# Four of a block's 123 weight splits moved from VectorE to GpSimd, in the first two attention slots of a decoder layer

## The reference

```python
mod = silu(c) @ ada_w + ada_b                       # shift, scale and gate of both halves
h = rms_norm(x, norm1_g) * (1 + scale1) + shift1
proj = h @ w_in                                     # attention q,k,v | deltanet q,k,v,beta,decay,z | gate A | gate D
o_attn = sliding_window_attention(q, k, v, sinks)   # window 128, 8 query heads, 2 key heads of 64
o_dn = gated_delta_rule(...)                        # 4 heads of 128; needs T = inverse(L + eye), L strictly lower
merged = sigmoid(gate_a) * (o_attn @ w_branch[A]) + sigmoid(gate_d) * (o_dn @ w_branch[D])
x = x + gate1 * (merged @ w_out)
h = rms_norm(x, norm2_g) * (1 + scale2) + shift2
x = x + gate2 * ((silu(h @ w_gate) * (h @ w_up)) @ w_down)
```

## Time and profile before

| what | value |
|---|---|
| median of three runs | 3070.0 us (3067.14 to 3070.06) |
| the profiled execution's own time | 3071.86 us |
| its span, first to last instruction | 3070.1 us |
| mean granted TensorE clock | 0.992 of full speed |
| TensorE matmul busy | 3010.6 us (98%) |
| VectorE / ScalarE / GpSimd busy | 53% / 39% / 4% |

### The profile page before, as it was taken

The page is one execution under the profiler, slowest core; times in us unless marked ns, Lnnn a source line. Parts: engine busy times, 40 slices in busy tenths (PEclk is TensorE's granted clock), DMA queues, the critical chain, the costliest instruction groups (busy, mean ns, idle before and its releaser), DMA issues.

```text
span 3070.1 us, 39395 instructions
## 1 busy us (share of the span) xinstructions
PE 3010.6 (98%) x15656; PEld 2477.8 (81%) x15656; DVE 1615.7 (53%) x2589; ACT 1211.3 (39%) x1980; POOL 114.1 (4%) x110
## 2 busy tenths in 40 slices
PE   7999999999999999999999999999999999999999
PEld 4887878888788788888879778888887977878887
DVE  4876565433466657333365756633336575643333
ACT  3654533222255544322245644422224554432222
POOL 0011000000001100000000110000000011000000
PEclk9999999999999999999999999999999999999999
DMA  6543344333434343333343344333334333323333
GB/s 250 162 151 100 127 158 151 96 96 100 134 104 127 98 130 115 105 96 96 97 137 123 97 116 143 102 98 97 96 95 137 128 107 100 124 83 96 96 96 103
DMA packets 138582, 358.30 MB, mean 117 GB/s; under 512 B 38304, under 2 KB 38560, under 8 KB 135328
## 3 DMA queue, kind: packets, MB, share of 16 engines
q1 hardware_dynamic: 134048, 347.40, 35.3%
q10 hardware_dynamic: 4352, 8.39, 0.7%
HBM read 326.38 MB, written 29.36 MB: 116 GB/s over the span
## 4 chain that ended last, share of the span: by engine, by line
PE 82%; DVE 7%; issue 4%; ACT 3%; DVEq 2%; DMA 1%; SPq 1%; POOL 0%; POOLq 0%; ACTq 0%
PE gb L1771 66%; PE gb L1800 4%; PE gb L2132 4%; PE mb L1977 2%; DVE w_lo L1152 1%; DVE tmp_c L1463 1%; DVE inv_c L1466 1%; PE mb L1972 1%; ACT sc L944 1%; PE mb L1950 1%; PE mb L1883 1%; ACT sc L936 1%; PE mb L2043 0%; DMA ada_buf<-in_ada_w 0%; PE gb L1782 0%
## 5 line engine op out<-in xcount | busy, mean ns | idle before, releaser
L1771 PE MATMUL gb<-h_hi,w_hi 128*128 128x512 f32 x2432 | 960.5, 395 | 18.6 <-DVE w_lo L1152 11.6
L1771 PE MATMUL gb<-h_hi,w_lo 128*128 128x512 f32 x2432 | 958.1, 394 | 0.0
L1771 PE MATMUL gb<-h_lo,w_hi 128*128 128x512 f32 x2432 | 958.1, 394 | 0.0
L752 ACT ACTIVATE w_hi<-w_raw 128x1024 fp32r<-128x1024 f32 x492 | 518.6, 1057 | 1040.7 <-PE gb L1771 981.3
L1152 DVE TENSOR_TENSOR w_lo<-w_raw,w_hi 128x1024 fp32r<-128x1024 f32 x492 | 600.7, 1222 | 485.0 <-ACT w_hi L752 483.7
L1771 PEld LDWEIGHTS gb<-h_hi,w_hi 128*128 128x128 f32 x2432 | 459.9, 189 | 120.6 <-DVE w_lo L1152 14.9
L1771 PEld LDWEIGHTS gb<-h_lo,w_hi 128*128 128x128 f32 x2432 | 460.3, 189 | 99.7 <-issue 6.5
L1771 PEld LDWEIGHTS gb<-h_hi,w_lo 128*128 128x128 f32 x2432 | 459.8, 189 | 95.8
L1771 PE MATMUL gb<-hid_hi,w_hi 128*128 128x512 f32 x704 | 274.0, 389 | 0.0
L1771 PE MATMUL gb<-hid_hi,w_lo 128*128 128x512 f32 x704 | 273.9, 389 | 0.0
L1771 PE MATMUL gb<-hid_lo,w_hi 128*128 128x512 f32 x704 | 273.9, 389 | 0.0
(11 more groups left out here) (287 smaller groups left out, 3350.2 us busy)
## 6 DMA issues: line engine op xcount, KB each, us to landing
w_raw<-in_wstream SPq DMA_DIRECT2D x492, 512.0 KB, 3.5
ada_buf<-in_ada_w SPq DMA_DIRECT2D x24, 1024.0 KB, 7.9
x<-in_x SPq DMA_DIRECT2D x4, 2048.0 KB, 10.1
out<-x ACTq DMA_DIRECT2D x16, 512.0 KB, 3.2
xs<-in_x SPq DMA_DIRECT2D x12, 512.0 KB, 5.8
scratch_nt<-st_nt SPq DMA_DIRECT2D x16, 256.0 KB, 2.5
scratch_at<-st_at SPq DMA_DIRECT2D x16, 256.0 KB, 2.9
scratch_kd<-st_kd SPq DMA_DIRECT2D x16, 256.0 KB, 3.1
```

Of the source, the lines that this page charges most:

```text
L752: act.activation(w_hi[s][:, :], w_raw[s][:, :], ACT.Copy).then_inc(w_high.sem, 1)
L1771: last = pe.matmul(bank(j), w, r, start=(i == 0), stop=(i == n - 1))
```

## The change

Units U_GATE + 3, + 4, + 7 and + 8 of every block get their low half from GpSimd, with the same subtraction on the same tiles. Each is counted by a semaphore of its own, w_pool; w_ready counts the others alone. Whoever waited for w_ready (SP's loads, TensorE's four kinds of unit) now waits for the one of the two that counts the unit in question. VectorE's `split` returns for these units and waits for nothing there. In GpSimd's list the four stand so: U_GATE + 3 + 4t ahead of invert_sum(t, 0), and U_GATE + 4 + 4t between invert_sum(t, 1) and attention_power(t + 1).

```diff
+POOL_LOW = (U_GATE + 3, U_GATE + 4, U_GATE + 7, U_GATE + 8)
+def low_by_pool(g):
+    return g % U_PER in POOL_LOW
+def lows_before(g, by_pool):
+    return sum(low_by_pool(n) == by_pool for n in range(g))
...
+    w_pool = nc.alloc_semaphore("w_pool")
...
+    def wait_low(eng, g):
+        if low_by_pool(g):
+            eng.wait_ge(w_pool, lows_before(g + 1, True))
+        else:
+            eng.wait_ge(w_ready.sem, RING + lows_before(g + 1, False))
...
             def load_unit(b, u):
-                sp.wait_ge(w_ready.sem, b * U_PER + (u + 1))
+                wait_low(sp, b * U_PER + u - RING)
...
+                def split_gate(g):
+                    u = U_GATE + g + 2
+                    s = (b * U_PER + u) % RING
+                    pool.wait_ge(w_high.sem, b * U_PER + u + 1)
+                    pool.tensor_tensor(w_lo[s][:, :], w_raw[s][:, :], w_hi[s][:, :].bitcast(fp32), ALU.subtract
+                                       ).then_inc(w_pool, 1)
                 attention_power(0)
                 for t in range(NT):
+                    if t < 2:
+                        split_gate(4 * t + 1)
                     invert_sum(t, 0)
                     invert_sum(t, 1)
+                    if t < 2:
+                        split_gate(4 * t + 2)
                     if t < 2:
                         attention_power(t + 1)
...
                 if b * U_PER + u >= NB * U_PER:
                     return
+                if low_by_pool(b * U_PER + u):
+                    return
...
-                    pe.wait_ge(w_ready.sem, w_ready.at(b, u + 1))
+                    wait_low(pe, b * U_PER + u)
```

## The result

The changed kernel takes 3087.5 us (median of five, 3082.1 to 3089.9) against 3070.1 for the kernel before in the same runs. The ratio is 1.0053, with a 95% interval of 1.0041 to 1.0065: 16.3 us slower by the ratio, where I had forecast 9.5 with 3084.5 as the upper end. The direction and the hold on VectorE were as forecast, the size was not. The profiled execution took 3088.32 us, with a span of 3086.6.

What follows compares the result with a forecast made beforehand. TensorE bounds the kernel, held in this stretch by two VectorE chains (masked probabilities; sweeps to images). Loss 2 x 3.2 + 2 x 1.75 = 9.9 us, set on the median: 3079.9, say 3079.5; range 3064.0 to 3084.5.

Steps and rivals of the forecast that it cites:

- GpSimd's duration: One GpSimd subtraction of 128 x 1024: 2.6 us, between 1.2 and 4.7, from three streams at a memset's rate.
- The hold for the whole subtraction: A VectorE sweep or subtraction beside a GpSimd subtraction waits until it ends; forecast case, chance 0.57, spanning 3075 to 3085.
- No hold: Rival: GpSimd's subtraction leaves VectorE running, only the root's 0.3 us stays; 5.6 us gained, 3064.4, chance 0.23.
- half a hold: Rival: the engines take turns within the instruction, sweeps lose 1.0 to 1.5 us; about 3072, chance 0.14.
- Lateness: Rival theory of the experiments: low halves and roots come later from the slower GpSimd, and that is all; no chance given.
- What can be held: VectorE beside GpSimd's subtractions: sweeps and subtractions with two SBUF inputs are held; masks reading PSUM are not.
- The second subtraction: Slot 0, U_GATE + 4: starts about 980.7 to 981.0, ends by 983.5, holds no masks; root behind makes VectorE 0.7 us late.
- Part A: Each block from the first turn of q to slot 2's first product; images and level_x forecast 3.2 us later.
- The wait after the removed one: Slot 1: TensorE's wait for U_GATE + 8's low half mostly goes; about 3 us for masked probabilities replaces it.
- The step that failed: Slot 2: level_x starts 3.2 us late; blocks 0 and 2 lose all of it, blocks 1 and 3 lose 1.75.
- parts B: Each block from slot 2's first product to the branch products; in blocks 1 and 3 a 1.4 us merge wait offsets lateness.
- The chances: Odds for the whole kernel against a 0.2% (6.1 us) threshold: slower 0.52, the same 0.36, faster 0.12.

Runs made afterwards that it cites:

- e6: The kernel before, with GpSimd also subtracting constants at the four places, result unused, all low halves still on VectorE: 3089.5 us, ratio 1.0063.
- e5: The changed kernel with GpSimd writing zeros for about as long instead of subtracting, the four low halves left out: 3071.2 us, ratio 0.9998 to the kernel before.
- e3: The changed kernel with only U_GATE + 8 made by GpSimd, the other three units back on VectorE: 3076.6 us, ratio 1.0019 to the kernel before.

## Why the prediction was right or wrong

- **GpSimd's duration**: taken as 2.6 us, measured 2.40, in 16 of 16 between 2.39 and 2.43. The working, three streams at a memset's rate, came within 8%; no run shows that the cost is made up so.
- **The hold for the whole subtraction**: right, shown by e6 against e5 and by the 2.36 to 2.54 us of held sweeps. *No hold* and *half a hold* fall. *Lateness* as the whole cause falls with e6.
- **What can be held**: incomplete. I counted instructions with two SBUF operands. A multiplication of 128 x 4 (2.40 us) and a copy of 128 x 8 (2.22 us), both with one, were held too. So the first hold delayed the maxima, and ScalarE's exponentials by 1.2 us, not only sweeps. A reduction from SBUF to SBUF was not held (0.69 beside a subtraction).
- **The second subtraction**: "The masks of the probabilities read PSUM and are not held" was right in blocks 0, 2 and 3. In block 1 it began 0.1 us before the last sweep of its group did, and held that for 2.54 us. VectorE then came to slot 1 later than in the other blocks by 0.3 to 0.6 us, just behind the start of the third subtraction instead of ahead of it. So that one held the copy for 2.22 us, where in the others maxima ran beside it and only 0.8 to 0.9 us were lost. The order was a matter of tenths of a microsecond, and my range had no case for it: block 1's part A grew by 4.8 us.
- **Part A**: predicted +3.2 us a block. Measured +3.0, +4.8, +3.3, +3.0. But for block 1 this term was right, and by the forecast route: in block 2 VectorE was late by 2.1 us behind the third subtraction (forecast 1.8), 1.0 after the removed one (0.65) and 3.1 at the end of the sweeps (3.2).
- **The wait after the removed one**: forecast of about 3 us before the masked products of slot 1 (L2007): 1.9 to 2.3, with 1.1 to 1.6 us more one step earlier, for the probabilities (L1995). At level_x I said 2.5 us or more: 3.2 to 3.7.
- **The step that failed** is the one on slot 2: "In blocks 1 and 3 TensorE used to wait 1.4 us more for a merge, whose own chain is late by 1.7: there the loss is 1.75", and in blocks 0 and 2 no more than the images' lateness. (Its 1.7 is 1.8 by its own numbers; nothing hangs on that.) Parts A and B together grew by 1.6, 7.2, 3.7 and 4.5 us in blocks 0 to 3, where 3.2, 1.75, 3.2 and 1.75 were forecast: the excess is in blocks 1 and 3. The wait for the merge did go, as said. But the longer wait at level_x was followed by TensorE at half clock: the parts B were to lose 2.9 us together and gained 2.85. That is 5.75 of the 7 us by which parts A and B exceed the forecast, and 5.4 of it is busy time for the same matmuls; block 1's holds in part A are the rest (1.3). e3's block 1 shows what I had taken for granted: no wait for the merge and full clock, 83.66 us, 1.4 under the 85.08 before. The trace of before had shown the other case, a mean clock of 0.96 behind the waits at level_x in blocks 0 and 2, and I had no term for it. Why a wait there is followed by the low clock in one block and not in another stays open.
- **The chances**: slower had 0.52. The range ended too low, since it had widened the subtraction only and not the cost of a wait.

## What to carry to other kernels

An instruction moved to GpSimd is not off VectorE if it reads SBUF: here sixteen subtractions held VectorE for some 24.7 us, up to 2.2 each, to save it 19.5, and the parts A of the four blocks grew by 14.1. Price a move by what VectorE will be issuing at that moment, and look first for the chain that sets the wait: here it was the sweeps and the images, and six matmuls put ahead of the image's first use gained 8.6 us by the ratio, more than the 5.6 forecast for the change without any hold. When a change lengthens a wait of TensorE, add a term for the clock behind it.

## What the runs showed of the hardware

- **The size of the held instruction plays no part.** A VectorE instruction of 0.17 us stood 2.40 us where a GpSimd subtraction began just before it. The Trainium skill, SBUF — State Buffer (Who interferes with whom), says that copies and tensor_scalar with one input may use both ports and contend, that outside those modes an instruction with at most one SBUF input does not contend, and that GpSimd's writes do not hold a two-input VectorE instruction. The trace agrees in all three: 2.22 and 2.40 us held, the masks, whose other input is in PSUM, at 0.67, and in e5 sweeps free with the multiplication held for 0.94.
- **A power on GpSimd holds next to nothing.** Its 1.95 us left sweeps at 0.33, while a subtraction of 2.4 held one throughout.
- **A wait can cost TensorE twice.** Stretches of the same 686 matmuls took 83.66, 86.62 and 87.53 us at a mean granted clock of 1.00, 0.96 and 0.95, the lower ones behind waits of 1.9 to 3.6 us. But a wait of 2.2 us in e3's block 1 had no such stretch behind it, and one of 1.9 in its block 2 had: the length of the wait alone does not decide.
